# A first gate/up step taken tile by tile: high weights first, low weights last

## What is computed

```
# layer 0 and 1
x = layer_norm(alpha * x + a.reshape(B, S, N_HEADS * HEAD_DIM) @ w_o[i], ln_mix_g[i], ln_mix_b[i])
f = swiglu(x, w_ffn_gate[j], w_ffn_up[j], w_ffn_down[j])        # (silu(x @ w_gate) * (x @ w_up)) @ w_down

# layers 2 and 3
h = _hybrid_mixer(h, ...)                                       # ends in mixed @ w_out
x = x + _rmsnorm(h, post_mix_norm[l])
h = _rmsnorm(x, pre_ffn_norm[l])
u = _causal_dwconv(h @ ffn_up, ffn_conv) + ffn_conv_bias
gate, val = jnp.split(u, 2, axis=-1)
h = (jax.nn.gelu(gate, approximate=True) * val) @ ffn_down
```

## Time and profile before

| | |
|---|---|
| median of three runs | 2226.89 us |
| span of the profiled execution (first to last instruction; no other time is given for it) | 2226.0 us |
| PE (TensorE matmul) busy | 2168.1 us, 97% |
| DVE (VectorE) busy | 1740.7 us, 78% |
| ACT (ScalarE) busy | 1425.6 us, 64% |
| chain that ended last | PE 86%, DVE 6%, ACT 4%, issue 2% |
| mean granted TensorE clock | 0.993 |

### The profile page before, as it was taken

How to read it: one execution, slowest core, us unless ns; L and a number is a source line. 1 busy time by engine, 2 the same in 40 slices (tenths; PEclk the granted TensorE clock), 3 DMA queues, 4 the chain that set the end, 5 groups by cost and what they waited for, 6 DMA issues and landing times.

```text
span 2226.0 us, 30778 instructions
## 1 busy us (share of the span) xinstructions
PE 2168.1 (97%) x11356; PEld 1812.4 (81%) x11356; DVE 1740.7 (78%) x1996; ACT 1425.6 (64%) x1590; POOL 54.6 (2%) x72
## 2 busy tenths in 40 slices
PE   8999999889999999999999999989999999999998
PEld 6688897668888888888888887779978898987888
DVE  7665567778888888888888889867677787776886
ACT  6544434757877777777777777656465556665654
POOL 2000000010000000000000003000000000000000
PEclk9999999999999999999999999999999999999999
DMA  9755554259999999999999999844135454224551
GB/s 392 255 188 190 189 186 178 101 212 393 360 405 369 379 380 377 375 372 388 365 387 363 396 352 399 340 160 150 67 124 202 176 200 145 94 105 151 190 186 61
DMA packets 82226, 573.25 MB, mean 258 GB/s; under 512 B 9600, under 2 KB 9712, under 8 KB 16800
## 3 DMA queue, kind: packets, MB, share of 16 engines
q1 hardware_dynamic: 76752, 545.82, 64.2%
q0 software_dynamic: 5376, 26.12, 3.2%
HBM read 564.03 MB, written 17.83 MB: 261 GB/s over the span
## 4 chain that ended last, share of the span: by engine, by line
PE 86%; DVE 6%; ACT 4%; issue 2%; DMA 1%; SPq 0%; ACTq 0%; DVEq 0%
PE bank L792 63%; PE bank L843 10%; PE bank L845 5%; ACT w_hi L529 2%; DVE w_lo L534 2%; PE bank L1125 1%; ACT arena L1457 1%; PE bank L1250 1%; PE bank L1260 1%; PE bank L1165 1%; DVE R L1991 1%; DVE arena L2004 1%; DMA raw<-in_wu_qkv 0%; PE bank L897 0%; ACT L529 0%
## 5 line engine op out<-in xcount | busy, mean ns | idle before, releaser
L534 DVE TENSOR_TENSOR w_lo<-raw,w_hi 128x2048 fp32r<-128x2048 f32 x506 | 1158.5, 2300 | 265.5 <-ACT w_hi L529 263.8
L529 ACT CAST w_hi<-raw 128x2048 fp32r<-128x2048 f32 x506 | 966.0, 1912 | 352.7 <-PE bank L792 262.0
L792 PE MATMUL bank<-w_hi,xT 128*128 128x512 f32 x2368 | 757.4, 395 | 12.3 <-DVE xT L1948 4.2
L792 PEld LDWEIGHTS bank<-w_hi,xT 128*128 128x128 f32 x2368 | 446.7, 189 | 118.6 <-DVE w_lo L534 11.1
L792 PE MATMUL bank<-w_lo,xT 128*128 128x512 f32 x1184 | 463.4, 391 | 0.0
L792 PE MATMUL bank<-w_hi,aT_hi 128*128 128x512 f32 x864 | 344.2, 398 | 2.4 <-DVE w_lo L534 2.4
L843 PE MATMUL bank<-xT,w_hi 128*128 128x512 f32 x960 | 341.1, 399 | 4.1 <-DVE xT L1948 2.9
L792 PE MATMUL bank<-w_hi,aT_lo 128*128 128x512 f32 x864 | 337.6, 391 | 0.0
L792 PE MATMUL bank<-w_lo,aT_hi 128*128 128x512 f32 x864 | 336.9, 390 | 0.0
L845 PE MATMUL bank<-xT,w_lo 128*128 128x256 f32 x960 | 270.1, 281 | 0.0
L792 PEld LDWEIGHTS bank<-w_lo,xT 128*128 128x128 f32 x1184 | 223.6, 189 | 44.1 <-issue 0.2
(11 more groups left out here) (339 smaller groups left out, 1696.6 us busy)
## 6 DMA issues: line engine op xcount, KB each, us to landing
raw<-in_wu_eg SPq DMA_DIRECT2D x112, 1024.0 KB, 7.2
raw<-in_wu_eu SPq DMA_DIRECT2D x112, 1024.0 KB, 7.2
raw<-in_wu_ed SPq DMA_DIRECT2D x112, 1024.0 KB, 7.2
raw<-in_wu_up SPq DMA_DIRECT2D x44, 1024.0 KB, 4.8
raw<-in_wu_ffn_gu SPq DMA_DIRECT2D x28, 1024.0 KB, 4.8
raw<-in_wu_in SPq DMA_DIRECT2D x28, 1024.0 KB, 4.9
raw<-in_wu_down SPq DMA_DIRECT2D x22, 1024.0 KB, 4.8
raw<-in_wu_ffn_d SPq DMA_DIRECT2D x14, 1024.0 KB, 4.8
```

Source lines behind the costliest of these rows:

```text
L529: nc.scalar.copy(w_hi[:, place(i), :], src).then_inc(*E.hi.mark("unit", i))
L534: nc.vector.tensor_tensor(w_lo[:, place(i), :], raw[:, i % RAW, :], w_hi[:, place(i), :].bitcast(F32), ALU.subtract) \
L792: mm = nc.tensor.matmul(o, l[i], r[j], start=(first and n == 0), stop=(last and n == 2), skip_group_check=not lone)
```

## The change

The first gate/up step of layers 0, 2 and 3 is written in a new form. `first_high(L, 0)` runs the 32 products of the high weights with tile 0 (high and low x side by side, 256 columns) between the transposes of tile 0 and those of tile 1, in place of the four warm-up matmuls in layer 0 and of two of the four in layers 2 and 3. `first_high(L, 1)` does the same for tile 1 once it is split, and `first_low(L)` ends the step with the 32 products of the low weights over both tiles. The transposes of the stage use banks 0 to 3, so that 4 to 7 are free for the step. On VectorE the low splits of the units (gu, 0, 0), (gu, 0, 1) and (gu, 1, 0) all stand behind the norm and the split of xT, and the split of tile 0 stands before the end of tile 1's norm. On ScalarE the squares of tile 0 in layers 2 and 3 stand before the cast of (gu, 0, 0).

```diff
-WARM_START, WARM_LN, WARM_RMS = 4, 4, 4
+WARM_START, WARM_LN, WARM_RMS = 4, 4, 2
@@ turn_bank
-            return (4 if stage[1] == "mix" else 0) + 2 * t + g
+            return 2 * g + t if stage[1] == "mix" else 2 * t + g
@@ PE
+            def first_high(L, t):
+                for i in range(2):
+                    n = unit_at["gu", L, 0, i]
+                    tile_ready((L, "mix"), t, (i,))
+                    pe.wait_ge(*M.hi.at("unit", key_of(n)))
+                    for half in range(2):
+                        for m in range(2):
+                            b = 4 + 2 * half + m
+                            o = open_bank(M, b) if i == 0 and t == 0 else bank[b]
+                            both = o[:, :].rearrange("p (a n) -> p a n", a=2)[:, :, t * P:(t + 1) * P]
+                            for kc in range(4 * i, 4 * i + 4):
+                                c0 = (kc % 4) * 512 + half * 256 + m * P
+                                nc.tensor.matmul(both, w_hi[:, place(n), c0:c0 + P], x_both[:, :, kc, t * P:(t + 1) * P],
+                                                 start=(kc == 0 and t == 0), stop=False, skip_group_check=True)
+
+            def first_low(L):
+                for i in range(2):
+                    key = ("gu", L, 0, i)
+                    u = unit(M, pe, key)
+                    for half in range(2):
+                        for m in range(2):
+                            for kc in range(4 * i, 4 * i + 4):
+                                c0 = (kc % 4) * 512 + half * 256 + m * P
+                                mm = nc.tensor.matmul(bank[4 + 2 * half + m][:, S:2 * S], u[1][:, c0:c0 + P], xT[0][:, kc, :],
+                                                      start=False, stop=(kc == KC - 1), skip_group_check=True)
+                        if i == 1:
+                            mm.then_inc(*M.groups.mark("gu", L, 0, half))
+                    name = ("gu", L, 0, 1) if i else ("unit",) + key
+                    if i == 0:
+                        mm.then_inc(*M.groups.mark(*name))
+                    released(M, unit_at[key], *name)
@@ PE, dense_ffn
-                    if s < n - 2:
-                        features(L, s, None if s else (L, "mix"))
+                    if s == 0:
+                        first_high(L, 1)
+                        first_low(L)
+                    elif s < n - 2:
+                        features(L, s)
@@ PE, layers 0 and 1
-                keep_warm(WARM_LN, 6)
+                if L == 0:
+                    first_high(L, 0)
+                else:
+                    keep_warm(WARM_LN, 6)
@@ PE, layers 2 and 3
-                keep_warm(WARM_RMS, turn_bank((L, "mix"), 1, 0))
+                keep_warm(WARM_RMS, 6)
+                first_high(L, 0)
@@ ScalarE, layers 2 and 3
+                sum_squares(L, "pre", 0, x_ready.at(L, "mix", 0))
                 walk("wo", L, 2)
-                sum_squares(L, "pre", 0, x_ready.at(L, "mix", 0))
                 walk("wo", L, 1)
                 half_squares(L, "mix", 1, wo_halves)
+                copy_T((L, "mix"), L, 0)
                 sum_squares(L, "pre", 1, x_ready.at(L, "mix", 1))
-                for t in range(NT):
-                    copy_T((L, "mix"), L, t)
+                copy_T((L, "mix"), L, 1)
@@ VectorE, layers 0 and 1
-                walk("wo", L, 2)
                 half_stats(0, 1, take_wo)
                 tile_normed(L, "mix", 4 * L, 0)
-                norm_tile(L, "mix", 4 * L, 1, take_wo)
-                for t in range(NT):
+                half_stats(1, 0, take_wo)
+                if L == 0:
+                    rest_T((L, "mix"), L, 0)
+                half_stats(1, 1, take_wo)
+                tile_normed(L, "mix", 4 * L, 1)
+                for t in range(1 if L == 0 else 0, NT):
                     rest_T((L, "mix"), L, t)
+                walk("wo", L, 2)
                 walk("wo", L, 1)
@@ VectorE, layers 2 and 3
             def enter_mix(L):
+                post_products(L, "mix", 4 + 2 * L, 1, wo_halves)
                 pre_turned(L, "mix", 0)
+                post_residual(L, "mix", 1, wo_halves)
+                rest_T((L, "mix"), L, 0)
                 pre_scale(L, "mix", "pre", 1)
-                rest_T((L, "mix"), L, 0)
                 pre_turned(L, "mix", 1)
                 rest_T((L, "mix"), L, 1)
@@
-                walk("wo", L, 2)
-                pre_scale(L, "mix", "pre", 0)
-                post_tile(L, "mix", 4 + 2 * L, 1, wo_halves)
-                enter_mix(L)
+                pre_scale(L, "mix", "pre", 0)
+                enter_mix(L)
+                walk("wo", L, 2)
                 walk("wo", L, 1)
```

More of the change, by code:

```diff
@@ L826, in first_part, with features @@
                     released(M, unit_at[key], *last)
-            def features(L, s, stage=None):
+            def first_high(L, t):
[28 more added lines that the diff above has]
+                    released(M, unit_at[key], *name)
+            def features(L, s):
                 for i in range(2):
                     key = ("gu", L, s, i)
-                    if stage:
-                        for t in range(NT):
-                            tile_ready(stage, t, (i,))
                     u = unit(M, pe, key)
```

## The result

The changed kernel takes 2237.38 us (median of four runs, 2235.45 to 2240.88) against 2227.51 us (four runs) of the kernel before: ratio 1.0049, 95% interval 1.0037 to 1.0062. It is 9.9 us slower. The prediction was 2236.4 us. The profiled execution has a span of 2237.2 us, 11.2 more than before. Busy time has hardly moved (before: PE 2168.1, VectorE 1740.7), so that is not where the time went.

A forecast was written before the change was run, and what follows sets the result against it. PE was taken as the bound, busy nearly the whole span. Layer 0 -0.7, layers 2 and 3 +3.9 each and clock +2.4 sum to +9.5 on 2226.0, 2235.5; the median lies 0.9 higher, 2236.4, range 2230 to 2242.

The forecast's parts named there:

- the stall with some drops: Main case: PE stalls before step 1 in layers 0, 2 and 3, with some clock drops; 2236.4 us, chance 0.58.
- High matmuls in the gap: Layer 0, step 0: tile 0's high matmuls run 94.31 to 98.15, before tile 1's transposes; tile 1's run 101.43 to 105.27.
- the upper bound of 0.14: Highest time in us assumed per 256-column high matmul over two halves of 128; it would add 1.3 us per layer.
- The stall: Before step 1, PE waits 2.96 us for bank sums behind the fourth low split, which awaits the first unit's late release.
- Rival A: Stall before step 1 does not form because the fourth split finishes while PE multiplies; -3.3 us, 2223.6, chance 0.07.
- Putting the later loads at nothing: Raw slots freed later delay unit loads by 4.8 us, counted as costing nothing; otherwise between 0 and 4.8 per layer.
- Layers 2 and 3: Gate/up entry: 1.9 us idle before high matmuls, later transposes, the stall and a 0.8 bank 6 wait; +3.9 us each.
- The clock: Clock may fall after each 3.0 us stall: 1.6 in layer 0, 0.8 in layers 2 and 3; three quarters taken, +2.4.
- rival C: Clock also falls inside the high matmuls after idle time before them, up to 1.6 us each; about 2241, chance 0.12.
- the prediction's reading of that rule: Transposes not counting as busy, layer 0's clock would drop for sure: 1.6 us more, 2238, chance 0.03.
- B: Clock stays up through all three stalls before step 1; +7.1 us, 2234.0, chance 0.18.
- D: Tile 0's high matmuls miss the gap and start only with tile 1's; +6.4 us, about 2243, chance 0.05.

The follow-up runs named there:

- experiment 1: Changed kernel, but in step 0 of layers 0, 2 and 3 corrections and bank sums precede the split of (gu, 1, 1): 2230.37 us, ratio 1.0021.
- experiment 5: Changed kernel with high tile 1 and low matmuls done for the first unit, then for the second, releasing the first mid-step: 2234.02 us, ratio 1.0041.
- Experiment 2: Kernel before with only the step's three-pass form (high tile 0, high tile 1, low); norm chain, tile order and four warm-ups unchanged: 2234.39 us, ratio 1.0037.
- experiments 6: Changed kernel with four warm-up matmuls instead of two before the high matmuls of layers 2 and 3: 2239.37 us, ratio 1.0058.
- 7: Changed kernel with bank sums before the split of (gu, 1, 1), and in layers 2 and 3 tile 0 split before VectorE's residual: 2226.75 us, ratio 1.0003.
- experiment 3: Change in layer 0 only, layers 2 and 3 as in the kernel before except the transposes' banks: 2227.97 us, ratio 1.0008.
- experiment 4: Change in layer 0 only, with step 0's bank sums before the split of (gu, 1, 1) there: 2223.42 us, ratio 0.9989.

## Why the prediction was right

**The forecast case, the stall with some drops, came in**: 2236.4 forecast, 2237.38 measured. By its own steps:

*High matmuls in the gap.* Layer 0: start forecast 94.31, came at 93.87; the whole program ahead of it was 0.34 earlier (91.80 for 92.14). Tile 1's transposes 99.26, came at 98.88; high tile 1 101.43, came at 101.00. With the shift, all within 0.1. The layout over two halves of 128 columns costs about what plain 256 columns cost: 32 in 3.94 (1658.33 to 1662.27 in experiment 1), 0.123 each, against the 0.12 taken; the upper bound of 0.14 is out.

*The stall.* Forecast 2.96, measured 2.88, 2.89 and 2.90. Its two links are shown: with the sums ahead of the split it is 0.40 (experiment 1), and with the first unit released earlier it is 1.01 (experiment 5). Experiment 2 shows that the norm chain has no part in it. Rival A is out, since the split did not overlap the matmuls. The low splits were in time, as forecast: the low matmuls follow without idle time. Putting the later loads at nothing held too: in the first 70 us behind down 0 PE waits for nothing in any of the three layers.

*Layers 2 and 3.* Idle before the first high matmuls forecast 1.9, measured 2.08 (1.72 in layer 3). VectorE's two multiplications stood 1.38 ahead of the residual (1661.64 - 1660.26), where 1.2 was forecast. The wait for bank 6 was forecast as 0.8 and is 0.58. Forecast +3.9 each; less the clock it came to +4.2 and +4.0 at down 0.

*The clock, the term that was mis-sized.* The sum had +2.4 for drops behind the stalls and, in layer 0's -0.7, the loss of a drop that was there before, -1.6: net +0.8. Measured in the three entries +3.6, and up to 5.5 over all runs. Behind the stalls the forecast was good: the clock fell in two of three layers and cost 1.5 and 0.7, 2.3 against 2.4, and over all profiles it fell in seven of ten, near the three quarters that were taken. What the sum lacked were drops inside the high matmuls, which I had left to rival C. They came twice in this profile (layer 0 tile 1, layer 2 tile 0), at 1.5 us each. Elsewhere it varies: layer 0's tile 1 fell in experiments 6 and 7 too and not in 1, 3 and 4; layer 2's tile 0 fell in none of 1, 5, 6 and 7. So C is not a case beside the forecast but something that some executions have. Its reading of why is refuted for the idle time: 2.08 us before the drop in layer 2, 2.07 in experiment 1 without one. What makes the difference stays open.

The Trainium skill (TensorE: Matmul & The Clock Gate, Part 4) says that a transpose in TensorE's transpose mode doesn't count as PE being busy in the same way. If layer 0's transposes are of that kind, the clock should always fall in its high tile 1, by the prediction's reading of that rule. It fell in this profile and stayed up in experiment 4, with the same transposes between idle times of 0.91 and 1.03 (100.61, 4.10 us for 32). So the rule does not settle it alone.

*Why the total agrees.* Forecast at full clock +8.7 (layer 0 +0.9, layers 2 and 3 +3.9 each), measured by the ledger +1.3, +4.2 and +4.0, +9.5. Clock +0.8, measured +3.6. Elsewhere 0, measured -1.9, which is scatter as far as I can tell: from layer 0's down 0 to the end of layer 2's projection the profiles run from 1528.6 (experiment 4) to 1534.1 us (experiment 3), and these two have the same code there. Their clock differs: length times (1 - granted clock), summed as in experiment 4 above, is about 7 us in the one and 14 in the other. It is about 12 both before and after, though, so the 1.45 us won there has no cause shown. The total is right to 1 us partly by luck: an undersized clock term was met by a favourable stretch. Set against this, the means over all runs divide it as 5.5 of clock and 6.1 of all else; the two accounts differ by some 3 us, more than one profile can settle.

*Rivals.* B, the clock up behind all stalls, isn't what the profile shows: 114.60 to 118.00 and 2056.80 to 2060.20 are at 0.51. D is out: the high matmuls ran before tile 1's transposes in each layer.

## What to carry to other kernels

When a step is reordered so that every pass uses both of its operands' buffers, the first buffer's release moves to the end of the step. Look up who waits for that release and what stands behind the waiter in its in-order queue; here the split of a later unit stood ahead of the sums that free PSUM banks, and 2.9 us of PE per layer went with it. Put the work that frees the bottleneck's banks ahead of the work that waits for the bottleneck, and then look at what you have put behind it: here the late split cost 0.8 us one step later in layers 2 and 3. And try such a change layer by layer. In layer 0, where it takes the place of warm-up matmuls, the timed runs are 2.6 us faster once the stall is gone; in layers 2 and 3 it wins nothing in any form tried.

## What the runs showed of the hardware

The granted clock does not follow from the schedule around it alone. The same 32 matmuls at the same place, behind the same idle time (2.08 and 2.07 us), took 5.60 us in one execution and 4.10 in another. A stall of 2.9 us was followed by a lowered stretch in layers 0 and 3 but not in layer 2 (step 1 keeps its 0.35 us for a pair there), and in seven of ten cases over all profiles; waits of 0.4 to 1.0 us at the same place in none of ten. Each lowered stretch shown above lasted 3.4 us. It cost 1.5 us in layer 0 and in layer 2's high matmuls, and 0.7 in layer 3, which had no wait for bank 6 where layer 2 had 0.58. Over many runs three stalls of 2.9 us go with a lower mean (0.9910, 0.9920 and 0.9907, against 0.9934 and 0.9937 before), so such a term should be sized from several runs, not from one trace.
